# Down projections with the high weights multiplied by the high and low activation in one 512-column matmul

## The chip, the cores and the metric

The kernel runs on 1 core of one Trainium2 chip. The metric is the device time of one execution in microseconds (us). The three runs of the kernel before gave 2317.76, 2319.73 and 2321.47 us.

## What is computed

One input `x` of 256 positions by 1024 features passes through two networks of two layers each. Ten blocks follow one another, and most of the time goes into matrix products in float32 accuracy. This change touches the last product of every feed-forward block and the last product of the recurrent block:

```python
# first network, per layer, for the context (layer 0 only) and for x:
u = dwconv1d(h @ w_up, dw, dw_b); a, g = split(u, 2)
x = x + g2 * ((silu(g) * a) @ w_down)              # 2816 -> 1024
# second network, two feed-forwards per layer:
g, u = split(h @ w_gu, 2)
x = x + 0.5 * (1 + gate) * ((silu(g) * u) @ w_down)   # 2816 -> 1024
# second network, layer 1, in between:
x = x + (1 + gate) * (y @ w_out)                   # 1280 -> 1024
```

There are seven feed-forwards (context layer 0, x layer 0, x layer 1, and four in the second network) and one recurrent output. Behind each of them stands an RMS norm of the new `x`, or (behind the context's and behind the first of x) one that belongs to the other stream.

## The kernel before, in words

**Data layout.** Features lie on the 128 partitions and the 256 positions along the free axis. Weights come in slabs: one slab holds the 128x128 weight blocks that make 128 output features (in the up projections 2 x 128), and is loaded in two halves (`raw`, two buffers `p` = 0, 1, two halves `f` = 0, 1). A chunk is one 128x128 block of weights with its 128 rows of activation.

**Three products per chunk.** Every float32 number is split in two parts of the type float32r. ScalarE makes the high weights (`split_hi`, L633), VectorE subtracts them from the raw ones and so makes the low weights (`split_lo`, L1166). The activation of a down projection lies in `e_both`, whose first half is `e_hi` and whose second half is `e_lo`. `mm3` (L1911 to L1913) then issues three matmuls of 256 columns for a chunk, all into the same 128x256 sums: high weights by high activation, high weights by low activation, low weights by high activation.

**Down stages.** The 22 chunks of a feed-forward's down projection are done in two stages of 8 slabs: part 0 has 12 chunks a slab, part 1 has 10. The recurrent output is one stage of 8 slabs with 10 chunks. That makes 7 x 8 x (12 + 10) + 80 = 1312 chunks in 120 slabs. Each slab is one output block of 128 features. Its sums stand in the first 256 columns of the first bank of `pb[p]`; `pb` has two pairs of banks, used by turns. When both halves of the slab are done (`half_done`), VectorE multiplies the sums by the gate column and adds them to the residual (`add_product`, L1634), which raises `updated`; that also frees the bank for the slab after the next.

**Order of the work.** Each engine has its own program, in the same order of stages; semaphores tie them together. The order on VectorE within a slab of a down stage is fixed by hand: the low weights of the next slab's second half, the low weights of the first half of the slab after it, the update of the residual, and then, where the stage has them, one product of the modulation weights (`mod_product`, L1194, 128x1024, with its own DMAs through GpSimd: `modraw` has two halves, and each is loaded again only when its product is done). Where a norm of the new `x` follows (`normed_body`), the update of slab j-1 is done in slab j, and after it come one addition of squares (L1337) and one low part of the next stage's first activation (L1281). In the stages ahead of a norm of the other stream (`norm_ahead`: part 1 of the context's feed-forward and of the first x feed-forward) the additions of squares lie in lumps behind the updates, and TensorE sums the squares in the middle of slab 3 (`norm_sum`, L1963). In the first stage of the second network (part 0 of its first feed-forward) VectorE also scales `x` once per slab (L1684).

ScalarE may write a half of `w_hi` again as soon as TensorE has finished that half of the slab two before (`half_done`); SyncE may load `raw` again as soon as VectorE has made the low weights from it (`lo_ready`). So the weights of the next slab's second half are split while a slab starts, and TensorE needs them one and a half slabs after that.

**The end of a stage with a norm behind it.** TensorE goes on with the next stage's first slab on an activation that lacks the norm's factor (`folded_half`, 258 columns: 256 positions and two columns of the shift), and after six chunks it sums the squares. For this it waits for the last slab's update on VectorE, its square on ScalarE (L948), and for the last blocks of this activation (L953, L1281). There are six such ends: the third x feed-forward, the four of the second network, one of them at the end of the program, and the recurrent output.

## Time and profile before

| | |
|---|---|
| median of three runs | 2319.73 us |
| span of the profiled execution | 2318.1 us |
| TensorE matmul busy | 2228.3 us (96%), 18082 matmuls |
| VectorE busy | 1837.1 us (79%) |
| ScalarE busy | 1308.9 us (56%) |
| mean granted clock of TensorE | 0.984 of full speed |
| DMA | 499.80 MB, mean 216 GB/s |

The profiled execution's span lies 1.6 us under the median; this is of the size of the spread of the runs, so the two are taken as the same execution with about 1.6 us around the span.

How to read what follows. A line of the timeline is start (us), length (us), engine, line of the kernel, instruction, names and shapes, and in brackets the idle time before it and what ended it. TensorE's rows show a matmul (PE) and its weight load (PEld) on their own; matmuls overlap one another in these rows (each lasts longer than the distance to the next), so the pace is the distance between starts. A line of a table of windows gives the busy time of each engine in a stretch, with the number of instructions in brackets.

### The profile page before, as it was taken

Reading aid. Unit: us, or ns where it says so; the run is one execution under the profiler, and the core shown is the slowest. Engines: PE = TensorE matmul, PEld = TensorE weight load, DVE = VectorE, ACT = ScalarE, POOL = GpSimd, SP = SyncE. Lnnn points to the kernel's source line nnn. Section 1 sums busy time; section 2 is a strip of 40 time slices with the busy share of each in tenths; the row PEclk is TensorE's granted clock in tenths of the full one; section 3 lists DMA queues with packets and bytes.
Section 4 is the critical chain, followed back from the end, with each engine's and each line's share of the span. In section 5 each row is a group of like instructions: output and inputs, shape, how many; then the busy total and the mean of one; then the engine's idle time right before and its main releaser. Section 6 shows DMA issues by size and latency. Waiting matters only on the chain.

```text
span 2318.1 us, 49499 instructions
## 1 busy us (share of the span) xinstructions
PE 2228.3 (96%) x18082; PEld 2145.7 (93%) x18082; DVE 1837.1 (79%) x3245; ACT 1308.9 (56%) x2142; POOL 119.9 (5%) x231
## 2 busy tenths in 40 slices
PE   7899999999999999999999999999999999979998
PEld 5798899998899999889999999988999999979998
DVE  4886866799789988978998878768877877878655
ACT  4366655536776554576665644657544644686443
POOL 0100000000000100000000001010001001000000
PEclk8999999999999999999999999999999999999999
DMA  9745676765358765534778687662777677635654
GB/s 360 243 143 188 231 243 203 257 200 172 116 172 276 266 229 199 174 119 163 241 261 281 230 272 265 212 224 82 236 276 264 227 278 267 229 118 178 227 168 132
DMA packets 150550, 499.80 MB, mean 216 GB/s; under 512 B 17408, under 2 KB 21632, under 8 KB 148864
## 3 DMA queue, kind: packets, MB, share of 16 engines
q1 hardware_dynamic: 113504, 374.01, 47.0%
q0 software_dynamic: 32544, 119.55, 16.3%
q10 hardware_dynamic: 4352, 4.20, 0.6%
q8 instruction: 99, 1.62, 0.3%
q14 instruction: 51, 0.42, 0.1%
HBM read 496.65 MB, written 1.05 MB: 215 GB/s over the span
## 4 chain that ended last, share of the span: by engine, by line
PE 71%; DVE 15%; ACT 6%; DMA 4%; issue 3%; ACTq 0%; SPq 0%; DVEq 0%; POOLq 0%; POOL 0%
PE bank_pair L1911 22%; PE bank_pair L1913 21%; PE bank_pair L1912 21%; DVE w_lo L1166 4%; DVE arena L1452 2%; DMA modraw<-in_w_mod 2%; ACT w_hi L633 2%; PE bank_pair L2034 1%; PE ps_o L1924 1%; DVE h_lo L1328 1%; DVE small L1528 1%; ACT arena L873 1%; DVE arena L1725 1%; ACT h_hi L718 1%; DMA e_plain<-in_w_mod 0%
## 5 line engine op out<-in xcount | busy, mean ns | idle before, releaser
L1166 DVE TENSOR_TENSOR w_lo<-raw,w_hi 128x1024 fp32r<-128x1024 f32 (+2 forms) x748 | 820.9, 1113 | 198.9 <-ACT w_hi L633 195.1
L633 ACT ACTIVATE w_hi<-raw 128x1024 fp32r<-128x1024 f32 (+2 forms) x748 | 714.2, 967 | 406.8 <-PE bank_pair L1913 274.3
L1911 PE MATMUL bank_pair<-h_hi,w_hi 128*128 128x256 f32 x2928 | 841.8, 287 | 13.3 <-DVE arena L1725 5.8
L1912 PE MATMUL bank_pair<-h_lo,w_hi 128*128 128x256 f32 x2928 | 831.4, 284 | 0.0
L1913 PE MATMUL bank_pair<-h_hi,w_lo 128*128 128x256 f32 x2928 | 831.3, 284 | 0.0
L1911 PE MATMUL bank_pair<-e_both,w_hi 128*128 128x256 f32 (+1 forms) x2064 | 593.0, 287 | 19.0 <-DVE e_both L1846 10.0
L1911 PEld LDWEIGHTS bank_pair<-h_hi,w_hi 128*128 128x128 f32 x2928 | 564.8, 193 | 35.5 <-issue 25.0
L1912 PE MATMUL bank_pair<-e_both,w_hi 128*128 128x256 f32 (+1 forms) x2064 | 587.4, 285 | 0.0
L1913 PE MATMUL bank_pair<-e_both,w_lo 128*128 128x256 f32 (+1 forms) x2064 | 587.2, 285 | 0.0
L1912 PEld LDWEIGHTS bank_pair<-h_lo,w_hi 128*128 128x128 f32 x2928 | 565.1, 193 | 0.3
L1913 PEld LDWEIGHTS bank_pair<-h_hi,w_lo 128*128 128x128 f32 x2928 | 564.8, 193 | 0.0
L1911 PEld LDWEIGHTS bank_pair<-e_both,w_hi 128*128 128x128 f32 x2064 | 399.0, 193 | 26.9 <-issue 16.7
L1912 PEld LDWEIGHTS bank_pair<-e_both,w_hi 128*128 128x128 f32 x2064 | 399.4, 194 | 0.3
L1913 PEld LDWEIGHTS bank_pair<-e_both,w_lo 128*128 128x128 f32 x2064 | 399.1, 193 | 0.0
L1194 DVE SCALAR_TENSOR_TENSOR modraw<-modraw,cact 128x1024 f32<-128x1024 f32 x174 | 211.9, 1218 | 20.2 <-DMA modraw<-in_w_mod 19.8
L588 POOL DMA_DIRECT2D modraw<-in_w_mod x216 | 114.1, 529 | 1997.7 <-DVE modraw L1194 1657.9
L1452 DVE SCALAR_TENSOR_TENSOR arena<-arena,par 128x256 f32<-128x256 f32 x360 | 149.8, 478 | 4.0 <-PE bank_pair L2254 3.8
L1725 DVE SCALAR_TENSOR_TENSOR arena<-bank_pair,par,arena 128x255 f32<-128x255 f32 x240 | 99.3, 477 | 40.1 <-ACT arena L1007 39.0
L1038 ACT ACTIVATE arena<-bank_pair 128x256 f32<-128x256 f32 x80 | 30.7, 383 | 114.2 <-PE bank_pair L1913 114.2
L1005 ACT ACTIVATE arena<-bank_pair,par 128x256 f32<-128x256 f32 x60 | 33.8, 564 | 104.1 <-PE bank_pair L1913 104.1
L1634 DVE SCALAR_TENSOR_TENSOR x_res<-bank_pair,cols,x_res 128x256 f32<-128x256 f32 (+1 forms) x128 | 60.6, 481 | 27.2 <-PE bank_pair L1913 25.8
L1760 DVE TENSOR_TENSOR arena<-bank_pair,arena 128x256 f32<-128x256 f32 x80 | 33.9, 424 | 48.7 <-ACT arena L1038 48.7
(264 smaller groups left out, 2176.2 us busy)
## 6 DMA issues: line engine op xcount, KB each, us to landing
modraw<-in_w_mod POOLq DMA_DIRECT2D x216, 512.0 KB, 4.9
raw<-in_w_gu SPq DMA_DIRECT2D x176, 512.0 KB, 4.6
raw<-in_w_up SPq DMA_DIRECT2D x132, 512.0 KB, 5.1
raw<-in_w_gate SPq DMA_DIRECT2D x48, 512.0 KB, 3.7
raw<-in_w_dn SPq DMA_DIRECT2D x64, 384.0 KB, 4.3
raw<-in_w_dn SPq DMA_DIRECT2D x64, 320.0 KB, 3.5
raw<-in_w_down SPq DMA_DIRECT2D x48, 384.0 KB, 5.0
raw<-in_w_down SPq DMA_DIRECT2D x48, 320.0 KB, 4.4
```

Of the source, the lines that this page charges most:

```text
L588: nc.gpsimd.dma_start(modraw[:, c, :], a["w_mod"][m, :, D * c:D * (c + 1)]).then_inc(mod_in[c], 16)
L633: nc.scalar.activation(w_hi[:, p, HALF * f:HALF * f + w], raw[:, p, HALF * f:HALF * f + w], ACT.Copy)\
L1005: nc.scalar.activation(scr[:, p, 0, :], z[:, 0, :], ACT.Identity, bias=fb[:, j, :], scale=taps[:, j, 1:2])
L1166: nc.vector.tensor_tensor(w_lo[:, p, at], raw[:, p, HALF * f:HALF * f + w], w_hi[:, p, at].bitcast(F32), ALU.subtract).then_inc(lo_ready, 1)
L1194: nc.vector.scalar_tensor_tensor(out=modraw[:, p, :], in0=modraw[:, p, :], scalar=1.0, in1=vector, op0=ALU.mult, op1=ALU.mult, accum_out=m ...
L1452: ins = nc.vector.scalar_tensor_tensor(out=o, in0=u, scalar=w[:, j, t:t + 1], in1=o, op0=ALU.mult, op1=ALU.add)
L1634: nc.vector.scalar_tensor_tensor(out=x[:, k, :], in0=pb[p][:, q, 0:T], scalar=cols[:, 2, :].unsqueeze(2)[:, k, :], in1=x[:, k, :], op0=ALU ...
L1725: nc.vector.scalar_tensor_tensor(out=o, in0=i_, scalar=taps[:, FC * q + j, 0:1] if left else taps[:, FC * q + j, 2:3], in1=o, op0=ALU.mult ...
L1760: ins = nc.vector.tensor_tensor(scr[:, p, 1, :], z[:, 1, 0:T], scr[:, p, 0, :], ALU.mult)
L1911: nc.tensor.matmul(out, l[0], r[0], start=start, stop=False)
L1912: nc.tensor.matmul(out, l[0], r[1], start=False, stop=False)
L1913: return nc.tensor.matmul(out, l[1], r[0], start=False, stop=stop)
```

## The change

In a down stage, a chunk now takes two matmuls. The first multiplies the high weights by the high and the low activation side by side: 512 columns, read from `e_both` as two blocks of 256, and written to the whole first bank (high product left, low product right). The second multiplies the low weights by the high activation (256 columns) into the right half. The residual then takes two updates in a row on VectorE, first the right half, then the left one; the second waits until the first is done (`low_added`), as both write the same block of `x`. All other products keep their three matmuls.

```diff
+                if s.kind == "down":
+                    nc.vector.scalar_tensor_tensor(out=x[:, k, :], in0=pb[p][:, 0, T:2 * T],
+                                                   scalar=cols[:, 2, :].unsqueeze(2)[:, k, :], in1=x[:, k, :],
+                                                   op0=ALU.mult, op1=ALU.add).then_inc(low_added, 1)
+                    dve.wait_ge(low_added, s.e0 + k + 1)
                 nc.vector.scalar_tensor_tensor(out=x[:, k, :], in0=pb[p][:, q, 0:T],
                                                scalar=cols[:, 2, :].unsqueeze(2)[:, k, :], in1=x[:, k, :],
                                                op0=ALU.mult, op1=ALU.add).then_inc(updated, 1)
...
+            def down_chunk(s, f):
+                return (FA if s.arg["part"] == 1 else 0) + s.kc // 2 * f
...
-                        ins = mm3(o, (w_hi[:, p, c:c + P], w_lo[:, p, c:c + P]), x, start, stop)
+                        if one:
+                            both = e_both[:, :, down_chunk(s, f) + k, :]
+                            nc.tensor.matmul(pb[p][:, 0, :].rearrange("p (e t) -> p e t", e=2), w_hi[:, p, c:c + P], both,
+                                             start=start, stop=False)
+                            ins = nc.tensor.matmul(pb[p][:, 0, T:2 * T], w_lo[:, p, c:c + P], both[:, 0], start=False,
+                                                   stop=stop)
+                        else:
+                            ins = mm3(o, (w_hi[:, p, c:c + P], w_lo[:, p, c:c + P]), x, start, stop)
```

## Rows read from the trace of the kernel before

**Rows 1.** Page, the chain that ended last by line, shares of the span.

```profile
PE bank_pair L1911 22%; PE bank_pair L1913 21%; PE bank_pair L1912 21%; DVE w_lo L1166 4%; DVE arena L1452 2%; DMA modraw<-in_w_mod 2%; ACT w_hi L633 2%; PE bank_pair L2034 1%; PE ps_o L1924 1%; DVE h_lo L1328 1%; DVE small L1528 1%; ACT arena L873 1%; DVE arena L1725 1%; ACT h_hi L718 1%; DMA e_plain<-in_w_mod 0%
```

**Rows 2.** Windows of down stages: us, PE, PEld, DVE, ACT, POOL busy, clock, DMA, GB/s.

```profile
1249.80:1278.60 28.80, 28.80 (x242) 28.80 (x241) 24.16 (x46) 19.83 (x36) 0.53 (x1) 1.00 0.76 250
...
1748.80:1783.40 34.60, 34.60 (x290) 34.60 (x289) 27.77 (x43) 13.93 (x18) 4.22 (x8) 1.00 0.84 286
1783.40:1812.20 28.80, 28.80 (x242) 28.80 (x241) 23.36 (x41) 18.55 (x32) 0.53 (x1) 1.00 0.77 248
```

**Rows 3.** Timeline of a down stage, TensorE at full clock, a chunk apart.

```profile
1959.94 0.28 PE L1911 MATMUL bank_pair<-e_both,w_hi 128*128 128x256 f32 x1
1959.94 0.19 PEld L1912 LDWEIGHTS bank_pair<-e_both,w_hi 128*128 128x128 f32 x1
...
1960.30 0.28 PE L1911 MATMUL bank_pair<-e_both,w_hi 128*128 128x256 f32 x1
```

**Rows 4.** Timeline, the same kind of matmul in a stretch of granted clock 0.50.

```profile
610.11 0.41 PE L1912 MATMUL bank_pair<-e_both,w_hi 128*128 128x256 f32 x1
...
610.96 0.41 PE L1913 MATMUL bank_pair<-e_both,w_lo 128*128 128x256 f32 x1
```

**Rows 5.** Timeline of a first slab, 258 columns, twelve matmuls apart.

```profile
2009.88 0.28 PE L1913 MATMUL bank_pair<-e_both,w_lo 128*128 128x258 f32 x1
...
2011.31 0.28 PE L1913 MATMUL bank_pair<-e_both,w_lo 128*128 128x258 f32 x1
```

**Rows 6.** Chain in order of time: 80 matmuls of 256 columns in plain float32.

```profile
487.75 17.28 PE bank_pair L2034 x80
```

**Rows 7.** Forms of TensorE's matmuls with `e_both` as the moving side, first of three.

```profile
L1911 PE MATMUL bank_pair<-e_both,w_hi 128*128 128x256 f32 x1776 | 509.3, 287 | 19.0 <-DVE e_both L1846 10.0 <-DVE e_both L1601 3.9 <-DVE w_lo L1166 2.7
L1911 PE MATMUL bank_pair<-e_both,w_hi 128*128 128x258 f32 x288 | 83.7, 291 | 0.0
```

**Rows 8.** Timeline of VectorE in part 0: updates of neighbouring slabs without idle time.

```profile
802.86 0.48 DVE L1634 SCALAR_TENSOR_TENSOR x_res<-bank_pair,cols,x_res 128x256 f32<-128x256 f32 x1
...
806.14 0.48 DVE L1634 SCALAR_TENSOR_TENSOR x_res<-bank_pair,cols,x_res 128x256 f32 x1
...
1417.14 0.48 DVE L1634 SCALAR_TENSOR_TENSOR x_res<-bank_pair,cols,x_res 128x256 f32<-128x256 f32 x1
...
1420.94 0.48 DVE L1634 SCALAR_TENSOR_TENSOR x_res<-bank_pair,cols,x_res 128x256 f32<-128x256 f32 x1
```

**Rows 9.** Timeline of VectorE in part 1 with a norm behind it.

```profile
1986.99 0.48 DVE L1634 SCALAR_TENSOR_TENSOR x_res<-bank_pair,cols,x_res 128x256 f32 x1
...
1990.33 0.48 DVE L1634 SCALAR_TENSOR_TENSOR x_res<-bank_pair,cols,x_res 128x256 f32 x1 [0.41 <-PE bank_pair L1913]
```

**Rows 10.** Timeline of VectorE: two operations, the second waits for the first.

```profile
843.67 0.42 DVE L1310 SCALAR_TENSOR_TENSOR arena<-ps_t,arena 128x256 f32<-128x256 f32 x1
844.13 0.42 DVE L1312 SCALAR_TENSOR_TENSOR arena<-arena 128x256 f32<-128x256 f32 x1
```

**Rows 11.** Timeline of VectorE in the context's down stage: modulation products.

```profile
430.65 1.23 DVE L1194 SCALAR_TENSOR_TENSOR modraw<-modraw,cact 128x1024 f32<-128x1024 f32 x1 [1.31 <-DMA modraw<-in_w_mod]
...
435.05 1.23 DVE L1194 SCALAR_TENSOR_TENSOR modraw<-modraw,cact 128x1024 f32<-128x1024 f32 x1 [1.30 <-DMA modraw<-in_w_mod]
```

**Rows 12.** Timeline, a stage's end with a norm: update, square, sum of squares.

```profile
2006.20 0.48 DVE L1634 SCALAR_TENSOR_TENSOR x_res<-bank_pair,cols,x_res 128x256 f32<-128x256 f32 x1
...
2006.71 0.42 ACT L948 ACTIVATE arena<-x_res 128x256 f32<-128x256 f32 x1 [1.69 <-DVE x_res L1634]
...
2007.18 0.70 PE L1963 MATMUL ps_t<-arena,tab 128*128 128x256 f32 x2 [0.20 <-ACT arena L948]
```

**Rows 13.** Timeline, the sum of squares in slab 3 of the stage at 827 us.

```profile
838.62 1.47 DVE L1337 TENSOR_TENSOR arena<-arena 128x256 f32<-128x256 f32 x3
...
840.15 0.70 PE L1963 MATMUL ps_t<-arena,tab 128*128 128x256 f32 x2 [0.36 <-DVE arena L1337]
```

**Rows 14.** Timeline of VectorE at a stage's end: idle time before the next weights.

```profile
1275.92 1.23 DVE L1166 TENSOR_TENSOR w_lo<-raw,w_hi 128x1024 fp32r<-128x1024 f32 x1 [1.46 <-ACT w_hi L633]
```

More of the change, by code:

```diff
@@ L432, in build @@
         dve_chain, act_chain = sem("dve_chain"), sem("act_chain")
-        updated = sem("updated")
+        updated, low_added = sem("updated"), sem("low_added")
         sq_ready, sq_added, sum_ready, log_ready, std_ready = (
```

## Prediction

> **What bounds the kernel now.** I read the chain that ended last first: the three matmul lines of `mm3` hold 64% of it, and no line of VectorE more than 4% [rows 1]. So a faster matmul is worth its full price wherever TensorE runs without a gap. Then I asked for windows over the down stages, to see whether they are such places. They are: over 34.60 us of a part 0 and over 28.80 us of two parts 1, TensorE is busy for the whole window [rows 2]. The stage lengths say the same: 8 slabs x 12 chunks x 3 matmuls = 288 in 34.6 us, and 8 x 10 x 3 = 240 in 28.8 us, which is 120 ns each. A slab is 4.32 us in part 0 and 3.60 us in part 1. VectorE is busy for 27.77 of 34.60 us and 23.36 to 24.16 of 28.80 us in the same windows [rows 2], so it is the second engine, and not far behind. The timeline gives the pace itself: from one chunk's first matmul to the next chunk's it is 0.36 us [rows 3].
>
> **What the 120 ns are.** The sum hangs on this. Before a matmul stands its weight load, which starts together with the previous matmul [rows 3], so two things run side by side and the longer one sets the pace. At the granted clock of 0.50 (1.2 GHz) the same matmuls are four starts in 0.85 us apart, 213 ns each [rows 4], and 256 columns at 1.2 GHz are 213.3 ns: there the columns are the bound, and nothing is added to them. At full clock (2.4 GHz) 256 columns would be 106.7 ns, but the pace is 120. Either a fixed 13.3 ns comes on top of the columns, or the weight load takes 120 ns of its own and the columns hide behind it. Two rows speak for the second. Matmuls of 258 columns do not cost more: twelve of them take 1.43 us, 119 ns each [rows 5], where columns plus 13.3 would give 120.8. And plain float32 matmuls of 256 columns, which at 213.3 ns would be two passes over them, run at 17.28 / 80 = 216 ns [rows 6], that is, the columns plus 2.7 ns and not plus 13.3.
>
> **The merged matmul.** No matmul here moves more than 258 columns [rows 7], so the price of 512 has to be bounded. From below: 512 columns at 2.4 GHz are 213.3 ns, and as 256 columns cost the full 213 at the low clock the columns can't be had for less. From above: two matmuls as they are now, 240 ns. I take 216, the row with as much streaming [rows 6]; the next value in reach is 213.3 + 13.3 = 226.7. The low weights' matmul behind it stays at 120, since the load of the next high weights starts only with it. A chunk is then 216 + 120 = 336 ns instead of 360, 24 ns less, and 1312 chunks give **31.5 us**. A slab becomes 4.03 us (part 0) or 3.36 us (part 1).
>
> The Trainium skill, page "TensorE: Matmul & The Clock Gate", section "LDWEIGHTS (loading the stationary operand)", gives a load as its columns by 1.2 GHz, an estimate of 107 ns for 128, which is near the 120 and independent of the moving columns; by "Back-to-back issue gap" an isolated matmul of 512 takes its columns plus 2.5 ns, an estimate of 216 that agrees with the row. The same section says that a stream of load and matmul pairs sustains about 131 ns per matmul at 512 columns. No row here shows that, and the low-clock row speaks against it.
>
> **VectorE: 120 more updates.** The added operation has the shape of the one that is there, 0.48 us. Where an operation waits for the one ahead of it, the next starts 0.46 us after it [rows 10]; in looped slabs some register work for the new wait may come on top, so 0.46 to 0.6, and I take 0.5. That is 60 us of work on VectorE, hidden wherever TensorE is still longer. Stage by stage:
> - Part 0 with modulation products: update to update without idle is 3.28 us [rows 8], so 3.8 us after, against 4.03. Hidden.
> - Part 0 of the second network's first feed-forward, with the scaling: 3.80 us [rows 8], so 4.3 against 4.03. VectorE falls 0.27 x 8 = 2.2 us behind.
> - Part 1 with a norm: 3.34 us less 0.41 idle is 2.93 [rows 9], so 3.43 against 3.36: 0.6 us behind over the stage. In the one ahead of the double norm (1249.80) it is 24.16 / 8 = 3.02 us on average [rows 2], with idle time at the stage's end [rows 14]; I take 3.2 for the rest, so 3.7 against 3.36: 2.7 us behind.
> Falling behind costs TensorE nothing at first. In a part 0, two splits lie between two updates, (3.28 - 0.40 - 1.2) / 2 = 0.85 us each [rows 8, 11]. The low weights of the next slab's second half are then ready 0.5 + 0.5 + 1.2 + 0.85 = 3 us into a slab, and TensorE wants them 1.5 x 4.03 = 6 us into it, so the cover is about 3 us. The bank has a whole slab of cover. But at the stage's end the last update stands directly on TensorE's way.
>
> **Where the updates are on the path.**
> - Six ends with a norm. Update (2006.20), square (2006.71), sum of squares on TensorE (2007.18) follow one another with nothing between [rows 12]. The second update comes 0.5 us later: 6 x 0.5 = 3.0 us.
> - What VectorE is behind at such an end comes on top, less its idle time there (1.46 us before one next load, [rows 14]): 2.7 - 1.5 plus some 0.6 for the end of the stage at 1250, 2.8 - 1.5 for the one after the scaled stage: together about 3.0 us. The other four: 0.25 each, 1.0.
> - Two norms ahead. TensorE already waits 0.36 us in slab 3 for the last additions of squares [rows 13]. In between VectorE has two more updates (1.0 us), and TensorE comes 1.5 slabs x 0.24 = 0.36 us earlier: 1.4 each, 2.7 us.
> - The context's part 0 is held by something else: its products wait 1.3 us each for their own DMA, and come 4.40 us apart [rows 11]. TensorE at 4.03 runs away from that by 0.3 to 0.4 a slab, so its gain of 8 x 0.288 = 2.3 us is lost behind the cover: 2.0.
> The sum of losses is 3.0 + 3.0 + 1.0 + 2.7 + 2.0 = 11.7, say 12 us, with 7 to 18 as its bounds: 7 if only the six ends, the two norms ahead and little else count, 18 if being behind also delays the loads (SyncE's load of `raw` is queued on `lo_ready`, so a late split makes the next load late).
>
> **Sum.** 2318.1 - 31.5 + 11.7 = 2298.3 us of span, and with the 1.6 us around it 2299.9. DMA traffic is the same; the stage at 1749 moves 286 GB/s at a share of 0.84 [rows 2], which becomes about 307 GB/s and 0.90.
>
> **Rivals.**
> - *A fixed 13.3 ns per matmul.* The merged one costs 226.7, a chunk saves 13.3 ns, 17.5 us in all. TensorE is then slower (4.16 and 3.47 a slab), VectorE falls behind less, and the losses are some 8 us: 2319.7 - 9.5 = 2310. For it: the pace at full clock alone. Against: 258 columns [rows 5] and the 216 ns [rows 6].
> - *Loads average out.* If the next high weights can be loaded under the 512 columns too, the low matmul takes 109 and a chunk 325: 46 us. VectorE then sets the pace in parts 1 (3.43 against 3.25) and the scaled stage, and losses are some 20: 2294. Against it: each load starts with the matmul before its own [rows 3].
> - *The columns are nearly free.* The merged matmul takes no longer than a load, 120 ns; a slab is then at most 12 x 0.24 = 2.88 us on TensorE and VectorE becomes the bound with 3.8 and 3.43 us: (4.32 - 3.8) x 8 + (3.60 - 3.43) x 8 = 5.5 us for each of seven, 38 in all, less 12 to 18 at the ends and in the scaled and the context's stage: about 2296. Against it: the low clock [rows 4]. The 131 ns of the Trainium skill's page "TensorE: Matmul & The Clock Gate", section "Back-to-back issue gap", would come out at the same time, since VectorE is the bound there too.
> - *The two blocks don't stream* (slower). The moving side is read as two blocks of 256 that lie 22 x 256 elements apart, and the product fills a whole bank; no row shows either. If the merged matmul costs the two it replaces, 240 ns, nothing is saved and the updates remain: 3.0 at the six ends, 2.0 at the two norms ahead (without the earlier TensorE), and 1 to 2 in the scaled and double-norm stages: 2319.7 + 6.5 = 2326. It decides from 240 - 6.5 / 1.312 = 235 ns upward.
> - *VectorE takes it back.* The merged matmul is at 336, but an update in a loop costs 0.7 us or more, or the lag feeds into the loads. Each 0.1 us on an update is 12 us of VectorE, of which parts 1 pass on nearly all (56 slabs, 5.6 us). With 0.7 the losses are about 25: 2313 to 2318.
>
> **Chances.** Forecast 0.55 (2300, its own range 2294 to 2306); fixed cost 0.18 (2307 to 2314); loads average 0.08; columns nearly free 0.02; VectorE takes it back 0.09 (half of it within 2315 to 2324); blocks don't stream 0.08. The range of 2290 to 2314 takes in the first four but for their edges and a part of the fifth, and leaves out about 0.17. A measurement of this kernel can tell about 0.2%, 4.6 us, from no change. Faster by over 0.2% (under 2315.1): 0.55 + 0.18 + 0.08 + 0.02 and a little of the fifth, 0.85. Within 0.2%: the rest of the fifth and the edge of the last, 0.08. Slower: 0.07. The clock adds a little noise: a stretch of 3.4 us at 0.50 costs 1.7 us, and these may fall elsewhere.
>
> **What the changed kernel's profile would show.** The start of the low weights' matmul 216 ns after the merged one's (226.7, or 240, for the rivals), and 120 ns on to the next. Slabs of 4.03 and 3.36 us in the two stages at 1749 and 1783, with VectorE busy 0.95 of them or more. Update to update 0.46 to 0.5 us. The sum of squares at each end 0.5 us or more later behind the last slab. In the context's part 0 slabs that stay near 4.3. The prediction is wrong if the first distance is not 216, or if TensorE has gaps inside the four part 0 stages of the second network.

## The result and the profile after

The changed kernel took 2338.8 us (median; its runs 2333.1 to 2342.4) beside 2320.6 us of the kernel before on the same chip. The ratio is 1.0077, with a 95% interval of 1.0061 to 1.0093: some 18 us **slower**. Forecast were 2299.9 us, a range of 2290 to 2314, and a chance of 0.07 for slower. The profiled execution has a span of 2337.3 us, against 2318.1.

From the page of the changed kernel, the busy time, share of the span and instructions of each engine:

```profile
PE 2226.8 (95%) x16770; PEld 2079.4 (89%) x16770; DVE 1885.9 (81%) x3365; ACT 1304.2 (56%) x2142; POOL 120.4 (5%) x231
```

VectorE is 48.8 us busier than before (1837.1), and TensorE's share of the span fell although it has less to do. Then the same three down stages as in [rows 2], in the changed kernel (columns as there):

```profile
1257.70:1288.10 30.40, 29.26 (x161) 24.37 (x160) 27.24 (x54) 18.36 (x36) 1.06 (x2) 1.00 0.75 244
1765.90:1799.80 33.90, 33.90 (x194) 29.43 (x193) 30.60 (x50) 13.94 (x18) 4.24 (x8) 1.00 0.85 292
1799.90:1828.10 28.20, 28.20 (x161) 24.46 (x160) 25.32 (x48) 17.11 (x30) 0.53 (x1) 1.00 0.77 240
```

The undisturbed part 0 fell from 34.6 to 33.9 us and part 1 from 28.8 to 28.2: a gain of 2%, not of the forecast 7%. The stage at 1257 became 1.6 us longer than it was, and TensorE is idle for 1.1 us of it. VectorE is busy for 0.90 of each stage. The pace itself, TensorE's timeline of the changed kernel:

```profile
1970.32 0.40 PE L2081 MATMUL bank_pair<-e_both,w_hi 128*128 128x512 f32 x1
1970.55 0.28 PE L2083 MATMUL bank_pair<-e_both,w_lo 128*128 128x256 f32 x1
1970.66 0.40 PE L2081 MATMUL bank_pair<-e_both,w_hi 128*128 128x512 f32 x1
1970.90 0.28 PE L2083 MATMUL bank_pair<-e_both,w_lo 128*128 128x256 f32 x1
1971.02 0.40 PE L2081 MATMUL bank_pair<-e_both,w_hi 128*128 128x512 f32 x1
```

On the average of the 176 chunks between 1957.8 and 2020.0 us the low weights' matmul starts 236.7 ns after the merged one and the next merged one 116.7 ns after that, which is 353 ns a chunk (a slab of 12 chunks takes 4.24 us, one of 10 takes 3.53). Forecast were 216 + 120 = 336. In the recurrent output alone the two distances are 230.0 and 116.8 ns, and a slab takes 3.47 us, 347 ns a chunk.

Where the time went is best seen in the list of TensorE's waits, summed over the whole kernel (what waits, for what: us in total, times, longest). The kernel before:

```profile
PE bank_pair L1911 <- DVE w_lo L1166: 9.9, 12, 3.0
...
PE ps_t L1963 <- DVE arena L1337: 5.4, 4, 3.8
...
PE ps_t L1963 <- ACT arena L948: 2.9, 6, 1.2
```

and the changed kernel:

```profile
PE ps_t L1968 <- ACT arena L948: 11.5, 6, 2.8
...
PE ps_t L1968 <- DVE arena L1337: 9.4, 5, 3.8
PE bank_pair L1916 <- DVE w_lo L1166: 7.9, 7, 3.0
...
PE bank_pair L2081 <- DVE w_lo L1166: 5.4, 6, 1.5
...
PE bank_pair L2081 <- DVE x_res L1639: 2.2, 2, 1.1
...
PE bank_pair L1916 <- DVE x_res L1639: 0.6, 1, 0.6
```

The sum of squares (L1963 before, L1968 after) waits 8.6 us longer for its square at the six ends, 4.0 us longer for the additions of squares, and the low weights are waited for 3.4 us more. The last two lines are waits for a bank that an update had not yet freed; the kernel before has none.

At one end with a norm, that of [rows 12], the changed kernel's timeline reads:

```profile
2017.97 1.06 ACT L633 ACTIVATE w_hi<-raw 128x1024 fp32r<-128x1024 f32 x1 [1.12 <-DMA raw<-in_w_lin]
2022.15 1.22 DVE L1166 TENSOR_TENSOR w_lo<-raw,w_hi 128x1024 fp32r<-128x1024 f32 x1 [0.47 <-ACT w_hi L633]
2023.29 0.48 DVE L1635 SCALAR_TENSOR_TENSOR x_res<-bank_pair,cols,x_res 128x256 f32<-128x256 f32 x1
2023.80 0.48 DVE L1639 SCALAR_TENSOR_TENSOR x_res<-bank_pair,cols,x_res 128x256 f32<-128x256 f32 x1
2024.32 0.42 ACT L948 ACTIVATE arena<-x_res 128x256 f32<-128x256 f32 x1 [2.21 <-DVE x_res L1639]
2024.79 0.70 PE L1968 MATMUL ps_t<-arena,tab 128*128 128x256 f32 x2 [1.91 <-ACT arena L948]
```

The pair of updates is 0.51 us apart, as forecast. But TensorE waits 1.91 us and not 0.20 + 0.5: the updates begin late, behind a split that ends 3.4 us after TensorE began the slab's last matmul. In the kernel before, where the update starts at 2006.20 us [rows 12], this was 2.2 us. The 1.2 us between them are VectorE's own lag: from 2010.69 us on it does one operation after another in its fixed order, idle for 1.4 us in all where it had been 2.3, and the load that ScalarE waits for here (1.12 us) does not hold it up, since VectorE is still at an update when the high weights are ready.

The worst place is slab 3 of the context's part 1. ScalarE and VectorE of the changed kernel:

```profile
441.36 0.72 ACT L633 ACTIVATE w_hi<-raw 128x640 fp32r<-128x640 f32 x1
445.39 2.33 ACT L633 ACTIVATE w_hi<-raw 128x640 fp32r<-128x640 f32 x3 [3.31 <-DMA raw<-in_w_down]
...
443.84 0.82 DVE L1166 TENSOR_TENSOR w_lo<-raw,w_hi 128x640 fp32r<-128x640 f32 x1
446.17 0.82 DVE L1166 TENSOR_TENSOR w_lo<-raw,w_hi 128x640 fp32r<-128x640 f32 x1 [1.51 <-ACT w_hi L633]
...
447.82 1.47 DVE L1337 TENSOR_TENSOR arena<-arena 128x256 f32<-128x256 f32 x3
...
449.35 1.22 PE L1968 MATMUL ps_t<-arena,tab 128*128 128x256 f32 x2 [3.10 <-DVE arena L1337]
```

and of the kernel before, in the same slab:

```profile
442.84 1.55 ACT L633 ACTIVATE w_hi<-raw 128x640 fp32r<-128x640 f32 x2 [1.32 <-DMA raw<-in_w_down]
...
443.61 0.83 DVE L1166 TENSOR_TENSOR w_lo<-raw,w_hi 128x640 fp32r<-128x640 f32 x1 [0.35 <-ACT w_hi L633]
```

Read them backwards: the sum of squares waits for L1337, which stands on VectorE behind a split; the split waits for ScalarE's high weights, and these for their DMA, 3.31 us where it was 1.32. SyncE issues a load of `raw` only when VectorE has split what lay in that half, so VectorE's lateness can come back to it through the load. The issue of the load in question, in the changed kernel and in the one before:

```profile
438.38 0.33 SPq L552 DMA_DIRECT2D raw<-in_w_down  x1
```

```profile
437.79 0.33 SPq L552 DMA_DIRECT2D raw<-in_w_down  x1
```

It is issued 0.6 us later, and ScalarE can start 7.0 us after the issue (445.39) where it was 5.05 (442.84). So 0.6 us of the lateness came through the issue, and some 2 us are a load that took longer to land. TensorE's clock fell within this pause, after some 2.4 us without a matmul. Windows of the changed kernel (the granted clock is the last figure but two):

```profile
441.60:448.60 7.00, 4.65 (x27) 3.75 (x25) 5.04 (x11) 3.55 (x5) 0.00 (x0) 1.00 0.63 207
448.60:455.40 6.80, 6.05 (x18) 5.10 (x19) 3.52 (x10) 2.06 (x4) 0.00 (x0) 0.50 0.39 127
```

For 6.8 us from 448.6 on, the clock is at the lower of its two levels (1.2 of 2.4 GHz). By the mean clock, 0.984 before and 0.981 after, such stretches sum to (1 - 0.984) x 2 x 2318 = 74 us and 89 us.

### The profile page after: what moved, and what is told of

It is laid out like the page before. It is cut to its first block, busy times and chain, and to the rows that moved or that the text cites. A ratio compares the mean times of both kernels' runs of the same rounds, so it can differ in the third digit from the quotient of the medians.

```text
span 2337.3 us, 47029 instructions
## 1 busy us (share of the span) xinstructions
PE 2226.8 (95%) x16770; PEld 2079.4 (89%) x16770; DVE 1885.9 (81%) x3365; ACT 1304.2 (56%) x2142; POOL 120.4 (5%) x231
## 3 DMA queue, kind: packets, MB, share of 16 engines
q8 instruction: 91, 1.49, 0.3%
## 4 chain that ended last, share of the span: by engine, by line
PE 65%; DVE 17%; ACT 7%; DMA 5%; issue 5%; ACTq 0%; DVEq 0%; POOLq 0%; SPq 0%; POOL 0%
PE bank_pair L1916 16%; PE bank_pair L1917 16%; PE bank_pair L1918 16%; PE bank_pair L2081 6%; DVE w_lo L1166 5%; DMA modraw<-in_w_mod 3%; PE bank_pair L2083 3%; DVE arena L1452 2%; ACT w_hi L633 2%; PE bank_pair L2043 1%; PE ps_o L1929 1%; DVE modraw L1194 1%; DVE x_res L1635 1%; DVE small L1528 1%; DMA raw<-in_w_down 1%
## 5 line engine op out<-in xcount | busy, mean ns | idle before, releaser
L2081 PE MATMUL bank_pair<-e_both,w_hi 128*128 128x512 f32 x1312 | 469.2, 402 | 17.6 <-DVE e_both L1851 10.0
L2083 PE MATMUL bank_pair<-e_both,w_lo 128*128 128x256 f32 x1312 | 369.8, 282 | 0.0
L2081 PEld LDWEIGHTS bank_pair<-e_both,w_hi 128*128 128x128 f32 x1312 | 248.5, 189 | 81.9 <-issue 13.6
L1916 PE MATMUL bank_pair<-e_both,w_hi 128*128 128x256 f32 (+1 forms) x752 | 221.7, 295 | 7.5 <-DVE e_both L1601 3.4
L1917 PE MATMUL bank_pair<-e_both,w_hi 128*128 128x256 f32 (+1 forms) x752 | 216.8, 288 | 0.0
L1918 PE MATMUL bank_pair<-e_both,w_lo 128*128 128x256 f32 (+1 forms) x752 | 216.7, 288 | 0.0
L1916 PEld LDWEIGHTS bank_pair<-e_both,w_hi 128*128 128x128 f32 x752 | 148.1, 197 | 14.7 <-issue 7.3
L1917 PEld LDWEIGHTS bank_pair<-e_both,w_hi 128*128 128x128 f32 x752 | 148.3, 197 | 0.4
```

The source lines that it names most:

```text
L1916: nc.tensor.matmul(out, l[0], r[0], start=start, stop=False)
L1917: nc.tensor.matmul(out, l[0], r[1], start=False, stop=False)
L1918: return nc.tensor.matmul(out, l[1], r[0], start=False, stop=stop)
L2081: nc.tensor.matmul(pb[p][:, 0, :].rearrange("p (e t) -> p e t", e=2), w_hi[:, p, c:c + P], both, start=start, stop=False)
L2083: ins = nc.tensor.matmul(pb[p][:, 0, T:2 * T], w_lo[:, p, c:c + P], both[:, 0], start=False, stop=stop)
```

## The experiments

Every ratio is to the kernel before on the same chip, whose median was 2319 to 2321 us throughout; a time without a ratio is that of a single run. The kernels were run on several chips, so small differences are read from the ratios and not from the times. A table at the end of this section holds TensorE's waits of nine of the kernels.

**The updates alone.** The high weights multiply the two activations in two matmuls of 256 again, into the two halves of the bank:

```diff
-  matmul(pb[p][:, 0, :].rearrange(...), w_hi, both, start=start, stop=False)
+  matmul(pb[p][:, 0, 0:T], w_hi, both[:, 0], start=start, stop=False)
+  matmul(pb[p][:, 0, T:2 * T], w_hi, both[:, 1], start=False, stop=False)
```

> VectorE's part alone: a chunk keeps its three matmuls of 256 columns, but the high-high product goes to the left half of the bank and the other two to the right half, and the residual takes the two updates. Theory (the merged matmul saves about 7 ns a chunk, 9 us in all, and the 120 added updates cost about 27 us): 2345 us, between 2338 and 2352. Rival (the loss is on TensorE, from writing whole banks or from the 512 columns, and the updates cost only the half microsecond at the six ends and some waiting): 2324 to 2330.

Measured: 2335.1 us, ratio 1.0065 [1.0044, 1.0087], with every matmul at 120 ns as before. Its clock was 0.985, not lower than before. It lies between the two expectations. So 120 updates of 0.52 us cost 15 us without any merged matmul: more than the 11.7 us that the forecast charged for everything.

**The matmul alone.** The added update is left out (and with it the right half's sums from the residual):

```diff
-                if s.kind == "down":
-                    nc.vector.scalar_tensor_tensor(... in0=pb[p][:, 0, T:2 * T] ...)
-                    dve.wait_ge(low_added, s.e0 + k + 1)
```

> TensorE's part alone: the merged matmul and the low weights' matmul as in the changed kernel, but only the left half is added to the residual (the products with the low parts are computed and left out of x). Theory: TensorE at 353 ns a chunk and no added update: 2320.6 - 9 = 2311.6, between 2308 and 2315. Rival: 2325 or more, with the gaps of the changed kernel still there.

Measured: 2317.5 us, 0.9991 [0.9973, 1.0008], above the 2308 to 2315 expected. The slabs are 4.24 and 3.53 us, so 1312 x 6.7 ns = 8.8 us were saved inside them, and only about 2 us arrived, with 4 us either way. One place where it is given back, TensorE's timeline of this kernel in the stage ahead of the double norm:

```profile
1260.09 0.49 PE L2076 MATMUL bank_pair<-e_both,w_hi 128*128 128x512 f32 x1 [1.68 <-DVE x_res L1634]
```

and ScalarE's, ahead of it:

```profile
1254.42 0.74 ACT L633 ACTIVATE w_hi<-raw 128x640 fp32r<-128x640 f32 x1 [3.05 <-DMA raw<-in_w_down]
```

TensorE comes to slab 3 and waits 1.68 us for the update that frees the bank. VectorE came to that update late: its split had waited 2.19 us for ScalarE's high weights, where it was 0.35 in the kernel before, and ScalarE 3.05 us for a load that had not landed. Then followed, as before, a chain of small operations for the second norm's columns. So a part of TensorE's gain is lost on loads, without any added work of VectorE. The kernel before has no such gap: TensorE is busy for all of [rows 2]'s first window.

**Part 0 alone, part 1 and the recurrent output alone.** The merged form with its update in only the one or only the other:

```diff
-                if s.kind == "down":
+                if s.kind == "down" and s.arg["part"] == 0:     # the other kernel: != 0
...
-                        if one:
+                        if one and s.arg["part"] == 0:          # the other kernel: != 0
```

> The change in part 0 of the seven feed-forwards only (56 slabs of 12 chunks), part 1 and the recurrent output as before. Theory: the slabs save 0.08 us each, 4.5 us, VectorE has room for the second update there (4.24 us a slab against 3.8), and no end with a norm stands behind these stages: 2315 to 2319. Rival (the loss is on TensorE): half of the 18 us, 2326 to 2332.

> The change in part 1 and the recurrent output only (64 slabs of 10 chunks), part 0 as before. Theory: 4 us saved, and nearly all of the 27 us of losses, which lie at the six ends, in the two stages with a norm ahead and the one before the double norm: 2338 to 2344. Rival: half of the 18 us, 2326 to 2332.

Measured: part 0 alone 2316.8 us, 0.9994 [0.9984, 1.0004]; part 1 and the recurrent output 2332.9 us, 1.0053 [1.0037, 1.007], less than the 2338 to 2344 expected. The loss sits where the squares, the low parts of the next activation and the ends are. The two together make -1.4 + 12.3 = 10.9 us, 7 less than the whole change; of this a few us are within the intervals, and the rest would be VectorE entering part 1 late from a part 0. It wasn't separated. The two also give the price of VectorE's time by stage. In part 0 the 56 updates are 29 us; with 4.5 us saved on TensorE and 1.4 left, they cost 3 us, a tenth. In part 1 and the recurrent output the 64 updates are 33 us; with 4.3 us saved and 12.3 lost, they cost 17 us, a half.

**What sets the merged matmul's pace.** Three kernels on the one without the added update: the 512 columns read as one contiguous piece; both matmuls with 512 columns; the low weights' matmul with 128. In all three `x` lacks the right half's sums. The first also takes the activation of a neighbouring chunk for the left half; the second adds the low weights' product to the left half too; the third leaves out half of the low weights' columns.

```diff
+  at = down_chunk(s, f) + k                                          # contiguous
+  pair = both if at == 0 else e_both[:, 0, at - 1:at + 1, :]
...
-  matmul(pb[p][:, 0, T:2 * T], w_lo[...], both[:, 0], ...)           # both 512
+  matmul(pb[p][:, 0, :].rearrange(...), w_lo[...], both, ...)
...
-  matmul(pb[p][:, 0, T:2 * T], w_lo[...], both[:, 0], ...)           # low 128
+  matmul(pb[p][:, 0, T:T + P], w_lo[...], both[:, 0, 0:P], ...)
```

> The merged matmul reads 512 columns that lie side by side (two neighbouring chunks of the high activation) instead of two blocks of 256 that lie 5632 elements apart; one update, so x lacks the low parts and gets wrong products on the right side: the time alone is wanted. If the two blocks are what makes the merged matmul 233 to 241 ns, a pair of matmuls falls from 353 ns to 333 to 336. If it is the width or the bank, the pair stays at 347 to 353.

> The low weights too multiply both halves (512 columns into the whole bank; one update, of the left half). If a matmul costs its columns plus a fixed 13.3 ns, a pair takes 453 ns; if the weight load of 120 ns is what a matmul of 256 columns waits for and 512 columns hide it, 432 ns; if 512 columns cost 233 to 241 whatever stands beside them, 466 to 482 ns.

> The low weights multiply only the first 128 columns (the rest of that product is left out; one update). If the load of the next weights takes 120 ns by itself, the pair stays at 347 to 353 ns. If a matmul is its columns plus a fixed cost, the pair loses 53 ns and takes 293 to 300.

Measured, contiguous: slabs unchanged at 4.24 and 3.53 us (2316.9 us in all). The two blocks are not what costs.

Both at 512 (2423.4 us in all), timeline of TensorE (the last row is six matmuls after the first):

```profile
1814.63 0.39 PE L2076 MATMUL bank_pair<-e_both,w_hi 128*128 128x512 f32 x1
1814.86 0.39 PE L2078 MATMUL bank_pair<-e_both,w_lo 128*128 128x512 f32 x1
...
1815.99 0.39 PE L2076 MATMUL bank_pair<-e_both,w_hi 128*128 128x512 f32 x1
```

1.36 / 6 = 226.7 ns each. That is 512 columns at 2.4 GHz, 213.3, plus 13.3: the same 13.3 that 256 columns have at 120. **At 512 columns 13.3 ns come on top of the columns**; they don't hide behind a load, as the forecast's 216 had it.

Low weights with 128 columns (2313.0 us in all), matmuls and two weight loads:

```profile
1759.64 0.19 PEld L2076 LDWEIGHTS bank_pair<-e_both,w_hi 128*128 128x128 f32 x1
1759.70 0.44 PE L2076 MATMUL bank_pair<-e_both,w_hi 128*128 128x512 f32 x1
1759.75 0.19 PEld L2078 LDWEIGHTS bank_pair<-e_both,w_lo 128*128 128x128 f32 x1
1759.98 0.22 PE L2078 MATMUL bank_pair<-e_both,w_lo 128*128 128x128 f32 x1
...
1760.04 0.44 PE L2076 MATMUL bank_pair<-e_both,w_hi 128*128 128x512 f32 x1
...
1760.72 0.44 PE L2076 MATMUL bank_pair<-e_both,w_hi 128*128 128x512 f32 x1
```

The merged matmul starts 60 ns after the low one (1759.98 and 1760.04), and as long after its own load (1759.64 and 1759.70), so a weight load does not hold it for 120 ns. The two loads follow each other by 0.11 us. But a chunk takes 1.02 / 3 = 340 ns, where columns plus 13.3 each would give 226.7 + 66.7 = 293, and where the other expectation was 347 to 353: neither was met. Half of the low matmul's columns gone saved 13 ns, not 53; the low matmul now starts 280 ns after the merged one.

**Fewer changes of width.** Again without the added update, the merged matmuls of a half slab first, then its low ones:

```diff
-  ins = matmul(pb[p][:, 0, T:2 * T], w_lo[...], both[:, 0], ...)     # behind each merged one
+  for k in range(n):                                                 # behind all of the half slab
+      ins = matmul(pb[p][:, 0, T:2 * T], w_lo[...], e_both[:, 0, down_chunk(s, f) + k, :], ...)
```

> As e2_matmul_alone (one update, right half left out of x), but within a half slab all merged matmuls stand first and the low weights' matmuls behind them, so that the width changes twice per half slab and not twice per chunk. If the 6.7 ns above columns plus 13.3 per matmul are the price of changing width, a chunk takes 347 to 348 ns (3.47 us for 10 chunks, 4.17 for 12). If they belong to the merged matmul as such, it stays at 353.

Measured: 2312.2 us in its one run; TensorE's timeline:

```profile
1959.92 1.55 PE L2076 MATMUL bank_pair<-e_both,w_hi 128*128 128x512 f32 x6
1961.30 0.88 PE L2083 MATMUL bank_pair<-e_both,w_lo 128*128 128x256 f32 x6
1962.02 1.32 PE L2076 MATMUL bank_pair<-e_both,w_hi 128*128 128x512 f32 x5
```

From 1959.92 to 1962.02 are six chunks in 2.10 us, 350 ns each; columns plus 13.3 would be 346.7, or 2.08. So about half of the 6.7 ns per chunk above 346.7 goes away. It is tempting to call the 6.7 ns the price of a change of width, but the same rows speak against it: the six low matmuls take 0.72 us, 120 ns each, and the six merged ones 1.38 us, 230 ns each, although no change stands between them. By the starts of all such neighbours in the stages from 1936.7 to 1997.9 us, a merged matmul behind a merged one comes after 232.3 ns, and a low one behind a merged one, where the width changes, after 228.5. The excess over 226.7 thus sits in the merged matmuls themselves. In the kernel with both at 512, which runs at 226.7, each activation is read twice in a row and here only once; whether that is the difference was not tested. What the excess is, why the pair of 512 and 128 pays most (340 - 293 = 47 ns), and why the recurrent output runs at 347 without grouping, is open.

**The dose of VectorE.** The added update is cut to 16 of 256 columns (the rest of the right half's sums is left out):

```diff
-  out=x[:, k, :], in0=pb[p][:, 0, T:2 * T], ... in1=x[:, k, :]
+  out=x[:, k, 0:16], in0=pb[p][:, 0, T:T + 16], ... in1=x[:, k, 0:16]
```

> The changed kernel with the added update on 16 of its 256 columns (the rest of the right half is left out of x); its wait and its place stay. Theory (it is the 0.5 us of VectorE's time per slab that makes splits and loads late): the added operation falls to some 0.2 us, so more than half of the updates' 15 us goes, 2321 to 2328. Rival (the second wait and its register work are what costs): it stays at 2333 or more.

VectorE's timeline of this kernel:

```profile
1961.99 0.23 DVE L1635 SCALAR_TENSOR_TENSOR x_res<-bank_pair,cols,x_res 128x16 f32<-128x16 f32 x1 [0.22 <-PE bank_pair L2083]
1962.26 0.48 DVE L1639 SCALAR_TENSOR_TENSOR x_res<-bank_pair,cols,x_res 128x256 f32<-128x256 f32 x1
```

Measured: 2328.1 us, 1.0027 [1.0011, 1.0043]. With the same TensorE program, VectorE gets 0, 120 x 0.27 = 32 and 120 x 0.52 = 62 us more, and the kernel takes 2317.5, 2328.1 and 2338.8: 10.6 and 21.3 us; by the ratios, which take out the difference between chips, 8 and 20. **About one third of the time added to VectorE arrives at the end**, and intervals of 4 us either way fit a straight line from the first microsecond on. A free part of a few us at the start is not excluded by them. A part of the third is TensorE's clock: the mean granted clock over the runs of the three kernels is 0.985, 0.983 and 0.982. (With TensorE as before it is a quarter: the updates alone cost 15 of 62 us.)

**The ends.** In part 1 and the recurrent output, the last two slabs are as before:

```diff
-                if s.kind == "down":
+                if s.kind == "down" and (s.arg["part"] == 0 or k < 6):
```

> The changed kernel, but the last two slabs of every part 1 and of the recurrent output are done as before (three matmuls, one update). If the ends with a norm are where the updates cost (the last update directly, and VectorE arriving late there), this gives back about 1 us at each of six ends: 2329 to 2334. If the loss is spread over the stages, it stays at 2336 to 2340.

Measured: 2335.5 us, 1.0066 [1.0046, 1.0085], about 3 us less than the change, which is within the intervals and just above the 2329 to 2334 of the first expectation. At five of the six ends of the table below the distance is still 1.4 to 3.1 us, because VectorE comes to them late; the last update itself is the smaller part.

**The products' loads.** The modulation loads fetch a quarter of their columns, in the changed kernel and in the one before; the other three quarters are zero:

```diff
-  dma_start(modraw[:, c, :], a["w_mod"][m, :, D * c:D * (c + 1)])
+  dma_start(modraw[:, c, 0:w], a["w_mod"][m, :, D * c:D * c + w])    # w = D // 4
```

> The changed kernel with the modulation loads from the 35th on cut to a quarter of their columns (the products run at full length on cleared columns, so most of the modulation is left out and the output is another): VectorE's work is the same, the DMA traffic of the down and up stages falls by 0.38 MB a product. If loads that land late, because the products' loads and the weights' loads compete, make the stalls of the parts 1 of the first network, the changed kernel is then within 10 us of the kernel before with the same cut. If VectorE's time alone makes them, it stays 15 to 18 us above it.

> The kernel before with the same cut of the modulation loads (most of the modulation is left out), as the partner of the run before this one. TensorE hardly waits for these loads in the kernel before: 2315 to 2320.

Measured: 2332.9 us, 1.0057 [1.0042, 1.0073], and 2319.2 us, 0.9999 [0.999, 1.0009]. The gap between the two kernels shrinks from 18 to 13.7 us. It is in neither expected range. Lighter loads are worth nothing to the kernel before and some 5 us to the changed one, though the intervals reach to nothing there too. A load of `raw` for part 1 of the first network takes a median of 3.4 us from issue to landing instead of 4.6, and at slab 3 of the context's part 1 TensorE's pause falls from 3.38 to 1.78 us. So the loads compete, but VectorE's added time is most of the gap.

**A faster TensorE on top of the updates.** The grouping, in the full change:

> The changed kernel with the grouped order in all down stages: TensorE gets another 6.7 x 1312 = 8.8 us of head start, VectorE's work stays. If VectorE and the loads behind it set the pace where the updates cost, most of this is given back: 2334 to 2340. If TensorE's share and VectorE's share simply add up, 2330.

Measured: 2340.9 us, 1.0093 [1.0073, 1.0113], not faster than the change, though its slabs are 4.20 and 3.51 us. At slab 3 of the first x feed-forward's part 1:

```profile
845.91 0.70 PE L1968 MATMUL ps_t<-arena,tab 128*128 128x256 f32 x2 [3.68 <-DVE arena L1337]
```

In the changed kernel this wait belongs to a pause of 1.92 us, here to one of 3.96. What TensorE saves, it waits here.

**A version that is faster than both.** The merged form only where VectorE has room: part 0 of five of the seven feed-forwards, without x layer 1's (it precedes the double norm) and without the scaled one; and the same with grouping.

```diff
-                if s.kind == "down":
+                if s.kind == "down" and s.arg["part"] == 0 and not scaled and not x_layer_1:
```

> The change only in part 0 of five feed-forwards: not in the one ahead of the double norm, nor in the scaled one, and in no part 1. There the slabs save 0.08 us each and no stage behind them is short of VectorE: 40 slabs, about 3 us. Theory: 2317, between 2314.5 and 2318.5 with the kernel before at 2320. Rival (TensorE's head start is lost in the part 1 that follows): no difference.

> e11_merged_where_free with the grouped order in the merged stages. If the grouped order brings 347 ns a chunk, 480 chunks save another 6.7 ns each, 3.2 us: 2312, between 2309 and 2315 with the kernel before at 2320. If it doesn't, as e11: 2315 to 2317.

Measured: 2315.3 us, 0.9983 [0.9972, 0.9993], and with grouping 2315.1 us, 0.9981 [0.9971, 0.9992]. The first is some 4 us faster than the kernel before, with 2 us either way; the grouping adds nothing that can be told.

**The waits side by side.** From TensorE's timelines: the distance (us) from the start of the last matmul ahead of the wait for the squares to the start of the one that waited, at the nine places where this sum stands in or behind a down stage. It is never below 0.46, and 0.58 holds a wait of 0.20 us [rows 12]. Each row is one execution; a single place varies by half a microsecond and more between kernels that don't differ there.

| kernel | context | x 0 | x 0, end | x 1 | b 00 | b 01 | b 10 | recurrent | b 11 | sum |
|---|---|---|---|---|---|---|---|---|---|---|
| before | 1.34 | 0.64 | 0.46 | 1.61 | 0.88 | 0.58 | 0.58 | 0.58 | 0.97 | 7.6 |
| after | 3.38 | 1.92 | 0.97 | 2.40 | 3.19 | 1.75 | 2.29 | 2.63 | 1.49 | 20.0 |
| updates alone | 2.53 | 1.67 | 0.97 | 3.02 | 3.19 | 1.10 | 1.10 | 2.13 | 1.49 | 17.2 |
| matmul alone | 1.75 | 0.73 | 0.46 | 2.71 | 0.83 | 0.65 | 0.79 | 1.53 | 0.97 | 10.4 |
| part 0 alone | 0.83 | 0.82 | 0.46 | 2.64 | 2.04 | 0.58 | 0.59 | 0.58 | 0.97 | 9.5 |
| part 1 alone | 3.24 | 1.78 | 0.98 | 2.44 | 2.26 | 1.18 | 1.88 | 2.79 | 1.49 | 18.0 |
| ends as before | 3.81 | 2.93 | 0.46 | 3.07 | 2.35 | 1.40 | 2.65 | 2.34 | 0.97 | 20.0 |
| light loads | 1.78 | 1.77 | 0.97 | 2.40 | 3.19 | 1.17 | 3.19 | 2.48 | 1.49 | 18.4 |
| merged where free | 1.09 | 0.64 | 0.46 | 1.11 | 0.90 | 0.58 | 1.30 | 0.58 | 0.97 | 7.6 |

## Why the prediction was wrong

The forecast was a gain of 31.5 us less losses of 11.7. Measured are a gain inside the slabs of about 9 us and losses of about 27. Both terms were mis-sized, and either alone would have left the forecast's range, the losses only just (2315 us).

**The failed step: what the 120 ns are, and with it the 216 ns for the merged matmul.** The prediction saw both readings, a fixed 13.3 ns on top of the columns or a load of 120 ns behind which the columns hide, and took the second. With both matmuls at 512 the pace is 226.7 ns, which is the price of the first reading, and the matmul behind the low one of 128 columns follows it after 60 ns, which a load of 120 ns would not allow. The rows taken as evidence did not carry it. [rows 6] are matmuls of another type, and what is added to them (2.7 ns) needn't hold for `fp32r`. [rows 5] tell of 256 against 258 columns and not of 512. And [rows 4], where nothing is added at the low clock, was read as if it told of the full clock. The first reading is not the whole either. All 817 distances within longer runs of 258-column matmuls in the kernel before average 119.9 ns, where columns plus 13.3 would be 120.8, and at the low clock nothing is added. So what sets the 120 ns at 256 columns stays open; shown is what 512 columns cost. With 226.7 a chunk is 226.7 + 120 = 346.7 ns, a gain of 17.5 us: the rival with 0.18. The chunk was slower still, 353.3, and the other 6.7 ns no row of before could have shown. That leaves 1312 x 6.7 ns = 8.8 us. The Trainium skill's page "TensorE: Matmul & The Clock Gate", section "Back-to-back issue gap", gives 216 ns (an estimate worked out from it) for an isolated matmul of 512 columns; the runs show 226.7 and, beside narrow matmuls, 236.7, and the measurement decides. The 131 ns of the same section did not show here either.

**The second failed step: the cover.** That the second update comes 0.5 us after the first was right (0.51 to 0.52). Wrong was that up to 3 us of being behind is free, so that only the last update of a stage counts, and that the bank has a whole slab of cover: TensorE waits for it three times in the changed kernel, 2.8 us in all. At the end of [rows 12] VectorE is 1.2 us further behind than before, where the forecast had 0.25, by its own work. The cover of 3 us had been worked out for a part 0, with two splits between two updates, and taken over to part 1. But part 1 costs half of VectorE's added time (17 of 33 us) and part 0 a tenth (3 of 29): where squares, low parts of the next activation and the chain of a second norm stand in VectorE's order beside the splits, the cover is used up.

The prediction names one way more, as a mere bound and as the 0.09 rival: a late split makes the next load of `raw` late, then the high weights, then the next split. In the context's slab 3 this gave 0.6 us of lateness, and some 2 us were a longer load. Over the second network, ScalarE's waits for the down weights seem to show it. The kernel before, the changed one, and the matmul alone:

```profile
ACT w_hi L633 <- DMA raw<-in_w_dn: 18.4, 11, 2.6
```

```profile
ACT w_hi L633 <- DMA raw<-in_w_dn: 40.2, 22, 3.1
```

```profile
ACT w_hi L633 <- DMA raw<-in_w_dn: 42.9, 24, 2.9
```

ScalarE waits for this DMA twice as often in the changed kernel and for 22 us more. But it does so without any added update too, so these waits come with a faster TensorE and are no sign of VectorE's lateness. That VectorE's added time costs is shown (the updates alone, +15 us with TensorE unchanged, and the dose); how much of it goes through the loads is not.

**Term by term.**
- *Six ends, 3.0 + 3.0 + 1.0 us.* Forecast were 7.0 together. Measured, the waits for the square rose from 2.9 to 11.5 us, 8.6. The six last updates at 0.51 us are 3.1 of it, as forecast; being behind is the other 5.5, where 4.0 were forecast.
- *Two norms ahead, 2.7 us.* The waits there grew by 2.04 and 1.28, 3.3 together: near. But the two stages lost more behind it: the context's part 1 became 5.3 us longer, at the lower clock for 6.8 us of it, with another pause of 1.4 us at its last slab.
- *Context part 0 held at 4.3 a slab, 2.0 us.* Wrong: its slabs were 4.24 us from the third on, and its products waited for their DMA only twice, 1.6 us in all, where it had been five times and 5.0 us; the loss came in its part 1.
- *Ahead of the double norm, 0.6.* The stage grew by 1.7 us and the time from there to the next down stage by 1.6. Part of this is no matter of the updates: the matmul alone shows a pause of 1.68 us there too, behind a load that landed late.
- *Scaled stage.* TensorE kept 4.24 in all slabs, as forecast; VectorE's lateness came out behind it, in a wait of 1.1 us for the bank in its part 1 and at the next sum of squares, 0.88 to 3.19.
- *The clock.* The prediction called it noise of a stretch or two. In its profiled execution the changed kernel has 15 us more at the low level, worth about half of that, 8 us. Four of its five longest distances in the table (3.38, 2.63, 2.40 and 2.29 us, not 3.19) have such a stretch beginning within 1.3 us of their end, 17 us together; with the updates alone three have one (2.53, 3.02, 3.19), in the kernel before none of the nine. So the pauses bring the clock down here, and a part of what they cost is paid behind them. How much is uncertain: the updates alone lost 15 us at a mean clock of 0.985, since that kernel had less of the low level elsewhere, and runs of the kernel before differ by as much among themselves.

**The account** for the two profiled executions, 19.2 us apart: waits for the sum of squares +12.4 (the table), for low weights +3.4 and for banks +2.8, the low clock about +8, the faster chunks -8.8. That is 17.8; 1.4 us are not assigned, and the losses overlap where a wait lies in a stretch at the low clock, so it closes only roughly.

**The rivals.** "A fixed 13.3 ns" had the price of 512 columns right where all matmuls have 512, was 10 ns short beside narrow ones, and wrong on its losses of 8 us (27), and so on the sign. The slower rival, "the two blocks don't stream", has the right side and nearly the right price: it decides from 235 ns upward, and the merged matmul took 236.7, though the chunk was 353 and not 360 ns. But the contiguous read shows its mechanism to be wrong, and its time of 2326 fell short because it kept the small losses of the forecast. "VectorE takes it back" is what happened, through its lag and not with an update of 0.7 us; it was held to 2313 to 2318 by a gain that wasn't there. With 226.7 and the loss that the forecast allowed as its upper bound, 18 us, the same sum would have given 2319.7 - 17.5 + 18 = 2320, no change. The two errors were not independent in effect: TensorE being faster, it waits more. The matmul alone gained 2 of 8.8 us, and the grouping on top of the updates gained nothing measurable. Whether a much larger gain on TensorE could have paid for the updates was not tested.

## What to carry to other kernels

When a change speeds up the busiest engine and loads the second one, price the second's added time at a measured share of it, stage by stage (here a tenth in part 0, a half in part 1, a third over all), not at zero up to a computed cover. A row of another data type, or one that compares widths close to each other, must not decide the price of a width twice as large; carry both prices to the end and look whether the sign holds. When a wait is to show a cause, look at it in the kernel without that cause: here ScalarE's waits for its loads grew just as much without the added updates. And apply such a trade only in the stages where the second engine has room: five parts 0 alone gave -4 us, where the whole gave +18.

## What the runs showed of the hardware that was not expected

- `fp32r` matmuls with a new weight block each take 120.0 ns at 256 columns and 226.7 at 512, which is the columns at 2.4 GHz plus 13.3 ns both times; but at 258 columns they take 119.9 and not 120.8. At the clock of 1.2 GHz nothing is added [rows 4].
- A stream of 512 and 256 columns in turn takes 353 ns against 346.7 (347 in one stage), 512 and 128 take 340 against 293. It is not the change of width: grouped by six, the merged matmuls still take 230 ns each, and the low ones 120.
- 512 columns read as two blocks of 256 far apart cost the same as one contiguous piece.
- The second of two dependent updates of 256 columns follows its first by 0.51 to 0.52 us; behind one of 16 columns it follows by 0.27 us.
- In the profiled executions of fourteen of the kernels, TensorE comes 2.2 to 4.0 us after its last matmul to the sum of squares 37 times; 25 of these pauses have a stretch of 3.4 or 6.8 us at the granted clock of 0.50 that begins within 1.5 us of their end. None of the nine distances of the kernel before (0.46 to 1.61 us) has one.
